# Storing each expert tile's result from ACT's DMA queue instead of GpSimd's, in a two-block transformer kernel

## The reference

```python
def hier_moe(x, ...):            # x: 512 tokens x 1024
    ...                          # each token gets one of 4 groups, and 2 of its 4 experts
    y = jnp.zeros_like(t)
    for e in range(N_EXPERTS):   # 16
        h = jax.nn.silu(t @ w_gate[e]) * (t @ w_up[e])      # 1024 -> 512
        y = y + gates[:, e:e + 1] * (h @ w_down[e])         # 512 -> 1024
    return y
h = h + hier_moe(rms_norm(h, ffn_norm), ...)
return rms_norm(h, final_norm)
```

## Time and profile before

| | |
|---|---|
| median of 3 runs | 1674.35 us |
| the profiled execution | 1678.19 us, of which its span is 1676.9 us |
| PE busy | 1492.6 us (89%) |
| DVE busy | 1042.8 us (62%) |
| ACT busy | 756.0 us (45%) |
| POOL busy | 136.7 us (8%) |
| DMA | 231.57 MB, mean 138 GB/s over the span |
| chain that ended last | PE 75%, DVE 15%, ACT 5%, issue 3%, DMA 1% |
| stores `result_rows<-osb` | 16 of 512 KB from POOL, 8.0 us median from issue to landing |

### The profile page before, as it was taken

How to read it: one execution, slowest core, us unless ns; L and a number is a source line. 1 busy time by engine, 2 the same in 40 slices (tenths; PEclk the granted TensorE clock), 3 DMA queues, 4 the chain that set the end, 5 groups by cost and what they waited for, 6 DMA issues and landing times.

```text
span 1676.9 us, 17418 instructions
## 1 busy us (share of the span) xinstructions
PE 1492.6 (89%) x6845; PEld 1163.3 (69%) x6845; DVE 1042.8 (62%) x1353; ACT 756.0 (45%) x994; POOL 136.7 (8%) x147
## 2 busy tenths in 40 slices
PE   3889949989988999999999999999988699999981
PEld 1666718857755788788887778786646578888861
DVE  5849976456333455445554648854443588898876
ACT  4453315564432422222223444235345568878763
POOL 5400000000000000000000022300000001111012
PEclk8898969989999999999999999999999799999996
DMA  5121204212210233232222222111002599999974
GB/s 194 63 75 51 75 26 148 74 55 75 76 50 17 106 142 114 75 113 101 101 69 69 102 100 76 51 51 51 26 1 88 215 352 413 410 410 414 407 310 176
DMA packets 41345, 231.57 MB, mean 138 GB/s; under 512 B 6448, under 2 KB 7728, under 8 KB 19120
## 3 DMA queue, kind: packets, MB, share of 16 engines
q1 hardware_dynamic: 29184, 198.75, 31.4%
q0 software_dynamic: 7584, 27.79, 4.4%
q10 hardware_dynamic: 4496, 3.91, 0.8%
HBM read 213.66 MB, written 16.78 MB: 137 GB/s over the span
## 4 chain that ended last, share of the span: by engine, by line
PE 75%; DVE 15%; ACT 5%; issue 3%; DMA 1%; ACTq 1%; POOL 0%; POOLq 0%; DVEq 0%
PE bank L415 14%; PE bank L416 14%; PE bank L417 14%; PE bank L2881 5%; PE bank L2883 5%; PE bank L2882 5%; PE bank L558 3%; DVE w_lo L371 2%; PE bank L434 1%; PE bank L2138 1%; PE bank L2167 1%; DVE bu L837 1%; PE bank L435 1%; PE bank L436 1%; PE bank L474 1%
## 5 line engine op out<-in xcount | busy, mean ns | idle before, releaser
L415 PE MATMUL bank<-h_hi,w_hi 128*128 128x512 f32 x952 | 393.9, 414 | 29.0 <-DVE h_lo L495 16.6
L416 PE MATMUL bank<-h_lo,w_hi 128*128 128x512 f32 x952 | 382.4, 402 | 0.0
L417 PE MATMUL bank<-h_hi,w_lo 128*128 128x512 f32 x952 | 382.0, 401 | 0.0
L371 DVE TENSOR_TENSOR w_lo<-w_raw,w_hi 128x2048 fp32r<-128x2048 f32 (+3 forms) x89 | 197.4, 2218 | 90.8 <-ACT w_hi L365 90.1
L415 PEld LDWEIGHTS bank<-h_hi,w_hi 128*128 128x128 f32 x952 | 183.8, 193 | 88.2 <-DVE h_lo L495 17.8
L417 PEld LDWEIGHTS bank<-h_hi,w_lo 128*128 128x128 f32 x952 | 183.7, 193 | 43.3
L416 PEld LDWEIGHTS bank<-h_lo,w_hi 128*128 128x128 f32 x952 | 184.3, 194 | 41.0 <-issue 1.9
L365 ACT ACTIVATE w_hi<-w_raw 128x2048 fp32r<-128x2048 f32 (+3 forms) x89 | 158.4, 1779 | 60.0 <-PE bank L417 60.0
L3061 DVE TENSOR_TENSOR h_lo<-w_raw,h_hi 128x2048 fp32r<-128x2048 f32 x32 | 73.2, 2291 | 15.4 <-ACT h_hi L2962 15.4
L3061 DVE TENSOR_TENSOR lo_b<-raw_b,hi_b 128x2048 fp32r<-128x2048 f32 x32 | 73.2, 2287 | 8.8 <-ACT hi_b L2962 8.7
L415 PE MATMUL bank<-a_hi,w_hi 128*128 128x512 f32 x176 | 69.4, 394 | 4.5 <-DVE a_lo L1579 4.5
(11 more groups left out here) (565 smaller groups left out, 2833.9 us busy)
## 6 DMA issues: line engine op xcount, KB each, us to landing
w_raw<-in_params_dram SPq DMA_DIRECT2D x122, 1024.0 KB, 4.9
raw_b<-in_params_dram SPq DMA_DIRECT2D x51, 1024.0 KB, 8.0
w_raw<-in_params_dram SPq DMA_DIRECT2D x16, 704.0 KB, 4.1
result_rows<-osb POOLq DMA_DIRECT2D x16, 512.0 KB, 8.0
result_rows<-prm POOLq DMA_DIRECT2D x8, 512.0 KB, 3.1
xt<-in_x_t_dram POOLq DMA_DIRECT2D x1, 2048.0 KB, 9.3
scratch_rows<-htm SPq DMA_DIRECT2D x4, 512.0 KB, 3.0
out_dram<-pr SPq DMA_DIRECT2D x4, 512.0 KB, 2.6
```

The costliest lines, as they stand in the source:

```text
L371: V.tensor_tensor(k.w_lo[:, g % SPLIT, 0:size], k.raw[:, g % RAW, 0:size], k.w_hi[:, g % SPLIT, 0:size].bitcast(F32), ALU.subtract).then_i ...
L415: PE.matmul(ps, wh, hi[:, c, 0:width], start=c == 0, stop=False)
L416: PE.matmul(ps, wh, lo[:, c, 0:width], start=False, stop=False)
L417: m = PE.matmul(ps, wl, hi[:, c, 0:width], start=False, stop=c == parts - 1)
```

## The change

The store leaves POOL's program for ACT's. In a fixed tile ACT issues it behind the second half of the result, and waits first until its own copy is complete (`m_act` has reached that event). In the loop it does the same. The semaphores `stored0` and `stored1`, the buffers and all other instructions stay.

```diff
-def pool_result(k, tile, i):
+def act_result_store(k, tile, i):
     dst = k.result_rows.rearrange("(n p) d -> n p d", p=P)
     dst = dst[tile, :, :] if type(tile) is int else ...
-    k.nc.gpsimd.dma_start(dst, k.osb[:, i, :]).then_inc(k.s.stored1 if i else k.s.stored0, 16)
+    k.nc.scalar.dma_start(dst, k.osb[:, i, :]).then_inc(k.s.stored1 if i else k.s.stored0, 16)
@@ pool_experts
         if c + 4 < E:
             rows(c + 4)
-        G.wait_ge(s.m_act, ACT_AT["o", 1, c])
-        pool_result(k, c, c % 2)
@@ pool_experts, in the loop
         G.wait_ge(s.pool_step, q + (k.g.n + 1))
-        G.wait_ge(s.m_act, q * len(ACT_LOOP) + (len(ACT_AT) + ACT_LOOP["o", 1]))
-        pool_result(k, q + FIXED, LOOP_BUFFER)
@@ act_experts, result(c, half)
         done(A.activation(k.osb[...], k.bank[DOWN[half]][:, :], ACT.Copy), "o", half, c)
+        if half:
+            A.wait_ge(s.m_act, ACT_AT["o", 1, c])
+            act_result_store(k, c, c % 2)
@@ act_experts, in the loop
         loop_result(1)
+        A.wait_ge(s.m_act, q * len(ACT_LOOP) + (len(ACT_AT) + ACT_LOOP["o", 1]))
+        act_result_store(k, q + FIXED, b)
         high(5)
```

## The result

| | median | runs |
|---|---|---|
| before | 1673.51 us | 6, 1671.64 to 1676.23 |
| changed | 1679.49 us | 6, 1678.81 to 1681.21 |

The ratio is 1.0037, 95% interval 1.0024 to 1.0050: the changed kernel is 6 us slower, where 0.1 us was forecast, and its time lies outside the forecast range of 1671.8 to 1677.6 us.

A forecast was written before the change was run, and what follows sets the result against it. PE was taken to bound the fixed tiles, with dependency chains at the loop's two ends. Terms 0, +0.6, +0.7 and -1.19 summed to +0.1 us on 1674.35, predicting 1674.5 us, range 1671.8 to 1677.6.

The forecast's parts named there:

- Fixed tiles, sum 0: 15 fixed tiles: store delays ACT's high part 5 by 0.57 us, idle time absorbs it, nothing reaches PE; cost 0.
- +0.6 ... All of it moves by 0.6: addition, gather, PE's start on the rows: Loop's start, after the last fixed result: the uncovered ACT delay passes through `tok_next` to PE, costing 0.6 us.
- the hold: Both POOL additions in the loop: each waits until DVE's low part ends; 2.22 us at the start, 0.18 with DVE idle.
- The clock, a rival at 0.03: Last two parts' matmuls: PE's idle grows to 1.7 us and its clock falls, costing +2.4 to +4.8 us; chance 0.03.
- The last tile, +0.7 - 1.19: Loop's end: 0.7 us more ACT delay, less 1.19 us that lay between DVE's last instruction and the results' first gather.
- DMA as the bound: Fixed tiles: three queues run less well, PE waits for loads; +4.6 us at 395 GB/s; chance 0.05.
- the issue: Store issue on ACT, taken as 0.35 us; rival: 1 us or so under busy DMA, sum +1.7 us; chance 0.06.

## Why the prediction was wrong

- **Fixed tiles, sum 0: right.** The delay was 0.58 us for 0.57; PE's pace and the DMA rate were unchanged, and the loads landed no later.
- **"+0.6 ... All of it moves by 0.6: addition, gather, PE's start on the rows": this step failed.** The addition moved by the delay, but the gather met DVE's second low part, which does not move along because its start hung on another wait. I used the hold twice, for the two additions, and did not ask it of the instruction behind the first, though the gathers of the fixed tiles showed it. The term was 0.6 and is 2.53: 0.58 of delay, 1.84 of hold, and a landing 0.11 later.
- **The clock, a rival at 0.03: it came about**, on the heels of the failed step. I had priced it for an idle time of 1.7 us. At 3.65 us the clock falls in the trace; at waits of 1.99 and 1.89 it did in one profiled execution each, 0.4 us after PE had started again; at 1.77, 1.68 and 1.56 it did not. It costs 3.5 us. That this lies within my 2.4 to 4.8 is partly luck: the price counted only the matmuls of the last two parts, and of the 3.4 us in the changed kernel's trace 1.3 are the twelve transposes, which I had left out, and 2.1 the matmuls.
- **The last tile, +0.7 - 1.19: right** in mechanism (the addition held 1.76 us by DVE's last low part) and near in size: from the last copy to the first gather of the results it is 6.11 us before and 5.66 after, -0.45 for the -0.49 of the sum. To the end of the span only -0.17 us is left; the gathers behind the first landed later in the changed kernel's profile (DVE waits 0.80 us for one), and why is open.
- **DMA as the bound: did not happen**, and the issue was not longer: 0.34 us in the fixed tiles for the 0.35 taken.

Sum: 2.5 + 3.5 - 0.2 = 5.8 us, where the runs say 6.2 (4.0 to 8.4).

## What to carry to other kernels

A delay of half a microsecond can turn round the order of two instructions on two engines, one of which holds the other up when it starts first. List, for each instruction that moves, what starts within that delay of it on the other engine. Where an engine issues a DMA behind work of its own, put the issue behind the next long instruction: the sequencer waits and issues while the arithmetic goes on. And compare two profiles from a common event close ahead of the place where they part, not by their spans.

## What the hardware showed beside

- A gather issued by POOL is held by DVE's low part (both inputs in SBUF), as the addition is. In the loop it took 2.84, 2.87 and 2.98 us where it started behind the low part, and 0.97 to 1.01 us where it started ahead, by as little as 0.09 us. The second low part took 2.29 us with a gather just under way (1631.53 in the kernel before), as the last one did with none: no run shows a gather that holds DVE.
- A plain store issued by POOL is not: 0.59 us at 1645.77, within DVE's low part of 1644.11 to 1646.40 in the kernel before.
- A store's issue on ACT took 0.34 us under DMA engines that were busy 99% of the time, beside 0.33 us for a load of 1 MB on SP.
